# Four row blocks instead of three, 32-token gather steps, and all V sums on TensorE, in a hybrid attention and expert-retrieval layer

## What is computed

```python
xn = rmsnorm(x); z = xn @ w_in            # conv B, C, h | q | k | v | two gates
a = (B * conv3(C * h)) @ w_conv_out       # causal, three taps
o = softmax(Q1 K1') V - lam * softmax(Q2 K2') V   # 8 heads, 64-row chunks causal
x = x + (sig(gA) * a + sig(gB) * rms(o) @ w_attn_out) @ w_o
xt = rmsnorm(x)
# retrieval: 8 heads, 128 x 128 product keys, the best 16 experts a head and token
h = gelu(dot(u[e], xt)); x = x + sum_k (g_k * h_k) * v[e_k]    # 128 experts a token
```

## Time and profile before

| what | value |
|---|---|
| median of 3 runs | 3985.5 us (3984.15 to 3986.57) |
| span of the profiled execution | 3979.7 us (the median of the runs is 5.8 us longer) |
| first dot product of a gathered row | 650 us |
| moved by DMA | 1340.72 MB, 1108.54 of it by the gathers |
| TensorE, VectorE busy | 3171.9 us, 2654.8 us |

### The profile page before, as it was taken

How to read it: one execution, slowest core, us unless ns; L and a number is a source line. 1 busy time by engine, 2 the same in 40 slices (tenths; PEclk the granted TensorE clock), 3 DMA queues, 4 the chain that set the end, 5 groups by cost and what they waited for, 6 DMA issues and landing times.

```text
span 3979.7 us, 46667 instructions
## 1 busy us (share of the span) xinstructions
PE 3171.9 (80%) x14264; PEld 1436.6 (36%) x14264; DVE 2654.8 (67%) x6242; ACT 1461.1 (37%) x4359; POOL 1531.1 (38%) x1405
## 2 busy tenths in 40 slices
PE   6999988788987999797788887876879666666655
PEld 3555545333433554353333333544425211111110
DVE  3443016988888964778677876885568864556664
ACT  2222001355654244223456564233323333333332
POOL 2111002355655433434445554442344443444333
PEclk9999999889998999898899988888889776776676
DMA  4223336799999999988789999999999999999998
GB/s 157 97 92 102 101 122 257 266 354 340 408 365 387 416 417 392 403 342 342 293 333 375 377 352 397 416 362 368 400 420 404 370 420 420 420 420 419 411 394 346
DMA packets 257065, 1340.72 MB, mean 337 GB/s; under 512 B 31472, under 2 KB 70128, under 8 KB 121392
## 3 DMA queue, kind: packets, MB, share of 16 engines
q0 software_dynamic: 152400, 1108.54, 69.3%
q1 hardware_dynamic: 79344, 204.15, 14.0%
q10 hardware_dynamic: 25072, 25.04, 1.8%
HBM read 1310.49 MB, written 27.15 MB: 336 GB/s over the span
## 4 chain that ended last, share of the span: by engine, by line
PE 42%; DMA 24%; DVE 17%; ACT 6%; issue 4%; DVEq 3%; SPq 2%; ACTq 1%; POOL 1%; POOLq 0%
DMA ringx<-in_peer_uv,tl_idx 12%; DMA mix<-in_peer_uv,tl_idx 11%; PE tl_ps L939 9%; PE tl_ps L991 8%; PE tl_ps L775 6%; PE tl_ps L974 4%; PE tl_ps L923 3%; PE tl_ps L950 3%; PE tl_ps L840 3%; DVE ringx L1610 3%; DVE mix L1610 3%; PE tl_ps L753 2%; DVE tl_xa L1621 2%; PE tl_ps L809 2%; SPq L611 1%
## 5 line engine op out<-in xcount | busy, mean ns | idle before, releaser
L701 POOL DMA_INDIRECT mix<-in_peer_uv,tl_idx x528 | 626.0, 1186 | 782.9 <-PE tl_ps L991 432.8
L701 POOL DMA_INDIRECT ringx<-in_peer_uv,tl_idx x528 | 612.7, 1160 | 731.7 <-PE tl_ps L991 450.8
L1610 DVE CUSTOM_DVE_ANT_0 mix<-mix,tl_xb 128x1024 f32<-128x1024 f32 x528 | 640.9, 1222 | 296.2 <-DMA mix<-in_peer_uv,tl_idx 288.3
L1610 DVE CUSTOM_DVE_ANT_0 ringx<-ringx,tl_xb 128x1024 f32<-128x1024 f32 x528 | 640.7, 1222 | 277.8 <-DMA ringx<-in_peer_uv,tl_idx 270.1
L991 PE MATMUL tl_ps<-ringx,tl_dg 64*64 64x512 f32 x3352 | 569.7, 764 | 298.8 <-ACT tl_dg L1235 298.3
L991 PE MATMUL tl_ps<-mix,tl_dg 64*64 64x512 f32 x3288 | 566.9, 775 | 280.3 <-ACT tl_dg L1235 256.7
L1224 ACT ACTIVATE tl_hg<-tl_hd 128x1 f32<-128x1 f32 x1056 | 213.3, 202 | 1560.9 <-DVE tl_hd L1610 1545.8
L939 PE MATMUL tl_ps<-tl_xr,low 128*128 128x384 f32 (+1 forms) x1280 | 401.9, 470 | 32.2 <-DMA low<-in_wall 27.7
L1228 ACT ACTIVATE tl_hw<-tl_hg,tl_gw 128x1 f32<-128x1 f32 x1056 | 310.9, 294 | 76.1 <-issue 4.6
L991 PEld LDWEIGHTS tl_ps<-ringx,tl_dg 64*64 64x64 f32 x3352 | 105.6, 155 | 639.4 <-ACT tl_dg L1235 566.8
L991 PEld LDWEIGHTS tl_ps<-mix,tl_dg 64*64 64x64 f32 x3288 | 104.9, 157 | 617.8 <-ACT tl_dg L1235 512.6
(11 more groups left out here) (193 smaller groups left out, 4002.1 us busy)
## 6 DMA issues: line engine op xcount, KB each, us to landing
low<-in_wall SPq DMA_DIRECT2D x240, 512.0 KB, 7.9
low<-in_watt SPq DMA_DIRECT2D x60, 512.0 KB, 9.0
mix<-in_peer_uv,tl_idx POOLq DMA_INDIRECT x528, 13.6
ringx<-in_peer_uv,tl_idx POOLq DMA_INDIRECT x528, 13.6
ringx<-in_watt SPq DMA_DIRECT2D x12, 512.0 KB, 5.9
tl_u<-in_x_prompt SPq DMA_DIRECT2D x8, 512.0 KB, 11.8
x_rows<-tl_u SPq DMA_DIRECT2D x8, 512.0 KB, 8.1
xs_rows<-tl_u SPq DMA_DIRECT2D x8, 512.0 KB, 7.5
```

The source lines that it names most:

```text
L701: nc.gpsimd.indirect_dma_start(out=ring[q % RING].rearrange("p a d -> p (a d)"), out_offset=None, in_=A["peer_uv"], in_offset=bass.Indirec ...
L1610: nc.vector.tensor_tensor_reduce(out=ring[q % RING][:, 0, :], in0=ring[q % RING][:, 0, :], in1=xb[:, t % 2, :], scale=1.0, scalar=0.0, op0 ...
```

## The change

`BLOCKS` becomes four blocks of 1, 2, 3 and 3 tiles (the last of 2 and the sample). Everything that counted in threes counts by `unit`, `place_of` and `TILES`. Block 0 is a unit a head, with all three of its conv blocks beside that unit, and `norms()` handles eight tiles instead of six. Block 1 is new: attention in slots 12 to 57, its middle from 57.7 to 104. Block 2's attention lies in slots 130 to 228 and its middle in 236 to 364, block 3's in 402 to 549 and 559 to 729.

A gather step takes 32 tokens and four of their experts each instead of 128 tokens and one: partition quadrant b holds the b-th expert of token r. So the index and gate tables are copied into that order (`by_quadrants`, 16 copies of 32 partitions for each table of a routing unit), `xb` holds 32 rows repeated four times (`load_row`, and `repeat_row` with three ScalarE copies a pass), and the V sum of a step gives 32 rows: four matmuls of 128 x 32 with 256 columns, one a quadrant of the output. `add_row`, `by_dve` and the diagonal of 64 go; every V sum is TensorE's. After 32 steps `add_sums` on VectorE adds the sum to `xa`, which holds the rows x1 by quadrant.

```diff
-BLOCKS = ((0, 3 * P, (0, 1, 2)), (3 * P, 3 * P, (3, 4, 5)), (6 * P, 2 * P + DEC, (6, 7, 8)))
+BLOCKS = ((0, P, (0,)), (P, 2 * P, (1, 2)), (3 * P, 3 * P, (3, 4, 5)), (6 * P, 2 * P + DEC, (6, 7, 8)))
...
-ATT = ((-330, 1.0), (25.5, 0.75), (337, 0.93))
+ATT = ((-330, 1.0), (12.0, 0.32), (130.0, 0.5), (401.9, 0.753))
...
-PLAN = ((-106.5, 1600, 1600, 7), (172.5, 1, 1750, 7), (520, 1, 1100, 7))
-CONV = (0, 24, 24)
+PLAN = ((-106.5, 533, 1343, 2.5), (57.7, 1, 4400, 2.5), (236.6, 1, 2173, 4.0), (558.9, 1, 1278, 5.8))
+CONV = (0, 24, 24, 24)
...
-SHARED = ((0,170,1,6),(170,300,3,4),(336,520,1,6),(520,680,2,3))
...
+def place(q):
...
+    t, k = divmod(q, SLOTS)
+    if t == 0:
+        return t, k // 8 % QUAD, k // 32 * 8 + k % 8
+    return t, k // TOKS, k % TOKS
...
             def weigh(q):
...
+                t, g, j = place(q)
+                pe.wait_ge(s["dg_done"], q + 1)
+                if q == 0:
+                    pe.wait_ge(s["n_cp"], REST)
+                elif j == (0 if t else 24) and QUAD * t + g > 1:
+                    pe.wait_ge(s["summed"], QUAD * t + g - 1)
+                for b in range(QUAD):
+                    last = nc.tensor.matmul(sums(g, b), dg[:, q % DIAGS, :], ring[q % RING][:, 1, b * COLS:(b + 1) * COLS],
+                                            start=j == 0 and g < 2, stop=j == TOKS - 1, skip_group_check=True)
                 last.then_inc(s["used_pe"], 1)
...
+            def repeat_row(p, b):
+
+                act.wait_ge(s["row_in"], 16 * (p + 1))
+                nc.scalar.copy(xb[quadrant(b), p % 2, :], xb[quadrant(0), p % 2, :]).then_inc(s["rows_done"], 1)
...
+            def by_quadrants(dst, src, t, h0, nh):
+
+                n = QUAD * nh
+                for g in range(1 if t == NT else QUAD):
+                    first = h0 // 2 * 32 + g * 8 if t == 0 else g * TOKS + QUAD * h0
+                    for b in range(QUAD):
+                        nc.vector.tensor_copy(dst[quadrant(b), t % 2, first:first + n], src[quadrant(g), b * n:(b + 1) * n])
...
+            def add_sums(q):
+
+                t, g, j = place(q)
+                dve.wait_ge(s["used_pe"], q + 1)
+                if g == 0:
+                    dve.wait_ge(s["xa_in"], 64 * (t + 1))
+                nc.vector.tensor_tensor(xa[:, g, :], ps[:, g % 2, g // 2 * COLS:(g // 2 + 1) * COLS], xa[:, g, :],
+                                        ALU.add).then_inc(s["summed"], 1)
```

More of the change, by code:

```diff
@@ L196, in _, with pass_length, sums_done @@
                 last.then_inc(s["tr_done"], 1)
-def by_dve(q):
+def place(q):
     t, k = divmod(q, SLOTS)
[L202 to L214, removed]
+    if t == 0:
+        return t, k // 8 % QUAD, k // 32 * 8 + k % 8
+    return t, k // TOKS, k % TOKS
+def pass_length(t):
+    return 8 if t == 0 else TOKS
+PASSES = [(k, 0, k // 8 % QUAD) for k in range(0, SLOTS, 8)] + [(k, k // SLOTS, k % SLOTS // TOKS) for k in range(SLOTS, NT * SLOTS + TOKS, TOKS)]
+PASS_AT = {first: p for p, (first, t, g) in enumerate(PASSES)}
+def sums_done(t, g):
+    return QUAD * t + g + 1
 def plan(rb):
@@ L580, in _ @@
             attend(0)
-            for rb in range(PASSES):
+            for rb in range(NB):
                 tiles = BLOCKS[rb][2]
@@ L748, in score @@
                     rows = [slice(c * HD, (c + 1) * HD) for c in range(2)]
-                    keys = [keys_of_unit(rb, par, rows[c], i, t) for c in range(2)]
+                    keys = [keys_of_unit(g, rows[c], i, t) for c in range(2)]
                     for j, (k, _) in enumerate(keys[0]):
@@ L1103, in store_heads @@
+                    act.wait_ge(s["tq_d"], unit(g, i) + 1)
+                    if i == 0 and old >= 0:
+                        act.wait_ge(s[f"kt_out{old % 2}"], stored_turned(old))
+                    nc.scalar.copy(qTh[:, at:at + n], ps[:, 6, 0:n])
+                    nc.scalar.copy(kTown[:, at:at + n], ps[:, 6, P:P + n]).then_inc(s["tq_c"], 1)
                 def store_heads(g):
-                    par, h = g % 2, g % DC
+                    par, h, first = g % 2, g % DC, own(g, 0)
                     cols = slice(h * P, (h + 1) * P)
-                    full = 3 if rb < 2 else 2
@@ new lines, in attend @@
+                units = DC * TILES[rb]
+                for u in range(-3, units + 1):
+                    g, i = place_of(rb, u)
+                    t = tiles[i]
+                    here = 0 <= u < units
+                    if u > 1:
+                        yield step_at(rb, u, TQ + 0.5)
+                        keep_out(*place_of(rb, u - 2))
+                    if 0 <= u + 1 < units:
+                        after = place_of(rb, u + 1)
+                        yield step_at(rb, u, TQ + 0.5)
+                        keep_heads(*after)
+                        if after[1] == TILES[rb] - 1:
+                            yield step_at(rb, u, TQ + 0.6)
+                            store_heads(after[0])
@@ L1441, in rotate @@
                 def rotate(g, i):
-                    n, j, half = rows_of(tiles[i]), 3 * g + i, HD // 2
+                    n, j, half = rows_of(tiles[i]), unit(g, i), HD // 2
                     dve.wait_ge(s["sq_d"], j + 1)
@@ L1508, in attend @@
+                units = DC * TILES[rb]
+                for u in range(-3, units + 1):
+                    g, i = place_of(rb, u)
+                    t = tiles[i]
+                    here = 0 <= u < units
+                    if rb == 0 and u > 0 and i == 0:
+                        yield step_at(rb, u, CV[2] + 1.8 - PERIOD)
+                        conv_taps(g - 1)
                     if here:
-                        yield step_at(rb, h, base + MX)
+                        yield step_at(rb, u, MX)
@@ L1628, in _ @@
             nc.vector.drain().then_inc(s["setup"], 1)
-            steps = [started(norms())] + [started(part(rb)) for rb in range(PASSES) for part in (attend, middle)] + [started(routing())]
+            steps = [started(norms())] + [started(part(rb)) for rb in range(NB) for part in (attend, middle)] + [started(routing())]
             for q in range(START, 0):
```

810 lines of the change are left out of this document (389 added, 421 removed).

## The result

The changed kernel takes 4066.15 us (median of 4 runs, 4063.36 to 4071.32), the kernel before 3984.82 us (4 runs). The ratio is 1.0206, 95% interval 1.0191 to 1.022: 2.1% slower, some 82 us, where 0.9% faster was forecast. The profiled execution has a span of 4069.5 us.

What follows compares the result with a forecast made beforehand. Limits were taken to differ by stage: TensorE until 650 us, DMA leading in attention, TensorE and DMA in middle 1, then DMA. Stage terms summed to 3944 us of span, plus 5.8: 3950 us, 0.9% less; range 3790 to 4110.

Steps and rivals of the forecast that it cites:

- The start: Start up to the first dot product: 305 us instead of 650, with bounds of 290 and 365.
- the V sum: A slot's sum on TensorE: four 128x32 tiles with 256 columns at once, 0.67 us instead of 1.09.
- the middles as TensorE's sum: Middle 1 (slots 57 to 104) and middle 2 (236 to 364) go by TensorE's work: 335 and 533 us.
- the stages from 549 on as DMA's: Slots 549 to 559, middle 3 and the gathers after 729 at DMA's pace: 26, 572 and 840 us.
- Rivals 2, 3 and 4: Rival 2: DMA sets every stage, 3820 us, 0.18; 3: V tiles run singly, 4425, 0.06; 4: start doesn't shrink, 4010, 0.07.
- The 48 us of slots 0 to 12: Twelve query blocks of tile 0 with one row of tiles, set by VectorE: 48 us.
- the estimate of about 0.8 us for four: V sum by the skill's rule: about 0.8 us, some 30 us on top in stages that TensorE sets.
- The step that failed: Attention 1, 2 and 3 (slots 12 to 57, 130 to 228, 402 to 549), near their largest load: 220, 340, 515 us.
- Rival 1: Attention units don't shorten, since each is a serial chain: periods 14, 14 and 20 us, 4110 us; chance 0.24.
- 32 small copies: Index and gate copies on VectorE in each routing unit: 0.12 us each, 4 us a unit.
- The 133 us of bytes: Block 1 reading all weights again: 54.5 MB, 133 us at 410 GB/s, counted among the gain given back.
- the forecast called itself wrong from 2060 on: Sign in the profile: dot 402 at about 1980 us; after 2060 (rival 1) or before 1850 the prediction is wrong.

Runs made afterwards that it cites:

- thin_all: The changed kernel fetching only an eighth of each weight block in all row blocks but the first: 4022.35 us, ratio 1.0114.
- three_blocks: The changed kernel's gathers, row copies and V sums, with the three row blocks, plan and attention paces of the kernel before: 4029.81 us, ratio 1.0136.
- thin_1: The changed kernel fetching only an eighth of each weight block in the second row block: 4061.04 us, ratio 1.0214.
- before_all_v: The kernel before with no V sum on VectorE, all on TensorE in the old form: 4038.72 us, ratio 1.0151.
- v_twice: The three-block kernel with each V sum of slots 25 to 170 and 337 to 520 added twice: 4044.38 us, ratio 1.0152.
- three_merged: The three-block kernel with index and gate copied together in one copy: 4033.96 us, ratio 1.0127.

## Why the prediction was wrong

**Right, with their sizes.** The start (305 forecast, 298), the weights nearly in time (TensorE waited 10.8 us for them between 66 and 298 us), the V sum (0.67 forecast; from 1412 to 1838 us, in middle 2, the 792 matmuls of 99 slots took 64.4 us, so 0.65), the middles as TensorE's sum within 5%, the stages from 549 on as DMA's. Rivals 2, 3 and 4 did not come. The 48 us of slots 0 to 12 are partly luck: the forecast put them on VectorE, and the stage has DMA at 1.01 and VectorE at 0.86. So is the time's place inside the range of 3790 to 4110 us: it moved the other way than was forecast. The terms given for middle 1 add up to 338 us, not 335, which changes nothing.

The Trainium skill ("TensorE: Matmul & The Clock Gate", Part 3, measured speedup) has 2.38x for three column tiles; the estimate of about 0.8 us for four that the prediction drew from it doesn't fit the 0.65 us measured here.

**The step that failed** is the one on the attentions, put as "three nearly equal loads will not do better than 1.03: 340 us" and followed by 1.05 over DMA and 1.13. In all three the largest measured load is the DMA's (its share times the stage), and against it they took 236 / 184 = 1.28, 374 / 337 = 1.11 and 552 / 486 = 1.14. The loads had been forecast well (194, 329 and 491 us); the factor over them was too small. Behind it stood the reading that the 0.93 DMA share in the earlier trace rows was the load that set attention. In the changed kernel it is not: thin_all took bytes away and attention did not move. What the runs show in its place is a chain of short pieces on TensorE, ScalarE and VectorE, none over 11% of it, in which work added to any of the three costs time; the stage can't be read as the maximum of the loads. That the written orders of the three engines set it, each waiting for the others, is the reading that fits these runs best; no run separates the order from the loads, so it is not shown. The three attentions are 87 of the 125 us between the forecast span (3944) and the measured one.

**Rival 1** named the place and not the mechanism. Periods came out at 11.8, 13.3 and 19.7 us, forecast 11, 12.1 and 18.4, the rival 14, 14 and 20: the third as it said, the first nearer the forecast. But work inside the unit's chain costs no more than the same work beside it (59 and 77 us), so the unit's chain alone, as the rival had it, is not what sets the period.

**What the forecast did not see is that the new form costs by itself.** It priced the new V sum for TensorE and took 289 us of add_row from VectorE. three_blocks shows what that exchange is worth: 172 to 337, where TensorE was the limit, 26 us longer; the stretches 0 to 104 and 337 to 520, 33 us longer; 559 to 729 14 us shorter; in all +48 us at the last dot. The part in the middle was in the forecast's own sum and not named as a loss: in middle 1 of the kernel before the V sums cost TensorE 87 us for 161 slots, since VectorE carried half of them; the new form costs 128 x 0.67 = 86 us for 128, and 447 + 86 = 533 was near the 550 measured. The part in the attentions was not in it; it belongs to the step that failed.

**The rest:** "32 small copies" at 0.12 us measured 0.178, which makes 34 us more of VectorE over 592 copies, part of it in the two routing gaps (24 us over) in which VectorE is 0.91 busy. Doing the copies twice cost 84 us, but moving or merging them won nothing over the whole kernel, so what they cost in place is not settled.

**The 133 us of bytes** that the forecast gave the fourth pass were a wrong reason: its own sum has slots 12 to 104 at TensorE and VectorE, so that these bytes are no term of it, and thin_1 shows that they are hidden. Some 310 us were to be given back of a start 345 us earlier; in the traces 442 were given back of 352. By slot 402 the start's 352 us of gain were spent (dot 402 at 2076 us, 2062 before; the forecast called itself wrong from 2060 on), on TensorE's 334 us for 47 slots in middle 1 and on the attentions.

**Left open:** why removing 46 us of copies from VectorE or some 88 from ScalarE wins nothing in all (8 to 15 us in slots 0 to 104, lost later), while added work costs 0.3 (ScalarE), 0.4 (TensorE) and 0.7 to 0.9 us (VectorE) a us. In the old form, taking 48 us of V sums from VectorE did make slots 0 to 104 and 337 to 520 13 us shorter in sum (before_all_v). The lower granted clock makes TensorE's steps in the chain longer (shown by v_twice); v_twice got the clock back and no time, so the clock is not all of it, or the doubled sums took as much as the clock gave. The part of the row copies and of the later index was not separated. The table loads before Gelus (135, and 106 in the kernel before) came with the fourth block, since three_blocks has 106 too; what they cost wasn't tested.

## What to carry to other kernels

In a stage whose chain is spread over three engines, don't forecast the maximum of the loads; take the ratio of time to work from the same kind of stage, and test it by adding work and by taking some away, since the two aren't symmetric. Where one engine is over 0.95 busy, its plain sum was right to 5%, and bytes beside it were free where DMA was at 0.77. Making a cheap thing cheaper on an engine that waits anyway can give nothing, and moving it there from a shared engine costs in every stage where the receiver is the limit.

## What the runs showed of the hardware

TensorE's granted clock went with its load in attention (slots 57 to 104): 0.95 in the kernel before with TensorE 0.85 busy, 0.88 with the lighter V sums and 0.76, 0.96 with them doubled and 0.82. The time of its fixed work went the other way: 578, 744 and 535 ns for the same score matmul, 86, 95 and 86 us for all of its work but the V sums. In the routing gaps the granted clock was 0.50 and 0.54, and from slot 729 on 0.51, with TensorE 0.42 busy there; the kernel before has 0.69 in that stretch.

On VectorE a copy of 32 partitions x 8 elements takes 164 to 174 ns and one of 32 x 16 takes 179 to 182 ns; in three_merged one of 32 x 32 takes 188 ns. Nearly all of it is fixed, so the number of such copies is what costs, not their size.
